# Routing the second head of the first expert group between the first five gathered rows

## The chip, the core and the metric

One NeuronCore of a Trainium2 chip runs the whole program. The time is the device time of one execution in microseconds; lower is better. The engines are called by their short names: PE is TensorE (matmuls and transposes), DVE is VectorE, ACT is ScalarE, POOL is GpSimd (here it issues the gathers), SP is SyncE (here it issues the plain loads and stores).

## What is computed

One inference step of a one-layer decoder: 256 prompt tokens and 8 x 4 sample tokens go through a recurrent head group, a sparse attention group, a cross-attention into 256 memory tokens and, last, a retrieval from 16384 single-neuron experts. The change lies in the last part and in the cross-attention of the second prompt tile. For every token and each of 8 heads the two halves of a query are scored against 128 keys, the 16 best of each half give 256 sums, the 16 best of these name 16 experts, and the rows of two tables are gathered by those numbers:

```
    qh = (x @ w_q).reshape(n, PEER_HEADS, 2, PEER_KEY_DIM)
    s = jnp.einsum('nhcd,hckd->nhck', qh, sub_keys).astype(jnp.float32)
    s1, i1 = lax.top_k(s[:, :, 0], PEER_TOPK)
    s2, i2 = lax.top_k(s[:, :, 1], PEER_TOPK)
    ...
    top_s, j = lax.top_k(cand, PEER_TOPK)
    e = jnp.take_along_axis(cidx, j, axis=-1)
    gate = jax.nn.softmax(top_s, axis=-1)
    h = jax.nn.gelu(jnp.einsum('nd,nhkd->nhk', x, u_tab[e]).astype(jnp.float32))
    return jnp.einsum('nhk,nhkd->nd', (gate * h).astype(x.dtype), v_tab[e])
```

## The kernel before

Tokens lie on the 128 partitions: prompt tile 0, prompt tile 1, and one tile of sample tokens. The expert part is cut into 9 groups (`NGRP`) of 32 picks (`PICK`), that is two heads of one tile each; groups 0 to 3 are tile 0, 4 to 7 tile 1, 8 the sample tokens. One pick is a "row": POOL gathers one row of `peer_u` for each of the 128 tokens (512 KB, 4 KB a token) into one of 6 slots (`USLOTS`), DVE multiplies it with the tokens and sums (L1327, result in `hcur`), and frees the slot (`u_free`). The rows of `peer_v` are gathered into 10 slots a group later, and PE adds them up with the weights `wz` (L1836), four rows a step.

Every engine has its own program, and the order on each is written out by hand. On DVE, PE, ACT and POOL a loop over a row number n runs beside the rest of the layer. On the first three it is a generator, `peer()`, and `stream.upto(step)` in the other code runs it until rows 0 to step - 1 are done. A table (`SIDE`) gives each piece of other work, called by its key, the row number at which it stands; `filled(engine, key)` and `pace(engine, key)` run the rows up to there and then wait for the key's bank. So ("mw", 1, c), the output projection of tile 1's cross-attention, stands at 13: rows 0 to 12 come ahead of it.

Routing a group (`experts`) is a generator too. It runs on DVE in small steps: `best16` on the scores, sums, `best16` again, then the expert numbers are put together by comparing with `iota16` (`eqm`, `ef`) and written as integers `Ei` (which POOL's gathers of u read) and four times as `E4`. Its arguments say which heads; with one head it has 25 steps. `e_half` tells POOL that head 0 of group 0 is there (rows 0 to 15), `e_ready` that the rest is. While the rows of group g are worked on, group g + 1 is routed between them, some steps a row.

The numbers for `peer_v` are needed turned: PE transposes `E4` into bank 2 and counts `et_full`, and DVE copies it into `ETi` (L1349) and counts `eti_ready`. POOL issues the gathers in one order: u0 to u16, v0, u17, v1, u18 and so on to v9, then u alone up to the second group. Ahead of v0 it waits for `eti_ready` and for the bank of ("mw", 1, 1), since the v slots lie over weights that this product reads.

The cross-attention of tile 1 runs in the same time: PE makes the scores ("ms", 1, k); DVE takes their maximum (`mem_max(1)`); ACT takes the exponentials straight from the banks (`mem_exps(1)`) and, behind that in its own order, the copies of the query block (0, 1) that PE waits for; DVE divides (`mem_weighted(1)`); PE turns the result, multiplies it with the values, and then with `w_mem_o` ("mw"). When ("mw", 1, 1) is done, SP loads the next 2 MB of `peer_w_q` into the same buffer, and the query block (0, 2) waits for that. `residual("mw", 1)` and `norm` on DVE end the cross-attention.

Of the kernel before, what the change touches and what calls it, by code (L numbers as in the profile page):

```python
# [38 lines left out]
NGRP = 9  # L39
# [260 lines left out]
def layer_kernel(nc, A, O):  # L300
# [145 lines left out]
    def vload(m):  # L446

        kind, k, use = V_PLACES[m][:3]
        return (s_u if kind == "u" else s_v)[k], 16 * use
# [79 lines left out]
    def bc(ap, axis, n):  # L529

        v = ap.unsqueeze(axis)
        shape = list(v.shape)
        shape[axis] = n
        return v.to_broadcast(shape)

    def split(ap, n):
        return ap.rearrange("p (a b) -> p a b", b=n)

    def toks(t):
        return TILES[t]  # L540
# [675 lines left out]
    def _(dve):  # L1216
# [99 lines left out]
        def peer():  # L1316

            route = None
            for n in range(NSTEP + PICK + 8):
                g, k = n // PICK, n % PICK  # L1320
                if n < NSTEP:
                    if n == 8 * PICK:
                        dve.wait_ge(s_rep, 48)
                    if k == 0 and g >= 2:
                        dve.wait_ge(gelu_done, g - 1)
                    dve.wait_ge(s_u[n % USLOTS], 16 * (n // USLOTS + 1))
                    v.tensor_tensor_reduce(out=uslot[n % USLOTS][:, :], in0=uslot[n % USLOTS][:, :], in1=xt[:, g // 4, :], scale=1.0, scalar=0.0,  # L1327
                                           op0=ALU.mult, op1=ALU.add, accum_out=hcur[:, g % 2, k:k + 1]).then_inc(u_free, 1)
                if 1 <= g <= NGRP:
                    o = g - 1  # L1330
                    if k == 1:
                        dve.wait_ge(gelu_done, o + 1)
                        if o >= 1:
                            dve.wait_ge(wt_full, o)
                        v.tensor_tensor(w4[:, :, :], bc(gcur[:, :], 1, 4), bc(Wg[:, o % 2, :], 1, 4), ALU.mult).then_inc(w4_done, 1)
                    if k == 3:
                        dve.wait_ge(wt_full, o + 1)
                        if o >= 2:
                            dve.wait_ge(v_done, 8 * (o - 1))
                        turned = bc(split(psum[:, 2, 128:256], 32), 1, 8)  # L1340
                        v.tensor_tensor(wz[:, o % 2], turned, bc(C("vmask", 32), 2, 4), ALU.mult).then_inc(wz_done, 1)
                if k == (10 if g else 12) and g < NGRP:
                    dve.wait_ge(et_full, g + 1)
                    if g >= 2:
                        dve.wait_ge(v_done, 8 * (g - 1))
                    for a in range(4):
                        rows = slice(32 * a, 32 * a + 32)
                        src = psum[rows, 2, 0:128].rearrange("p (j i a) -> p a i j", j=4, a=4)[:, a]
                        v.tensor_copy(ETi[rows, g % 2, :].rearrange("p (i j) -> p i j", j=4), src).then_inc(eti_ready, 1)  # L1349
                if g < NGRP - 1:  # L1350
                    start, last, each = (17, 24, 6) if g == NGRP - 2 else (4, 20, 3)
                    if k == start:
                        route = experts(g + 1)
                    if start <= k < last:
                        for _ in range(each):
                            next(route, None)
                    if k == last:
                        for _ in route:
                            pass
                    if n == 10:  # L1360
                        gates(0)
                    if k == 30:
                        gates(g + 1)
                for t in range(2):
                    if n == 4 * PICK * (t + 1) + PICK + 4:
                        dve.wait_ge(v_done, 32 * (t + 1))
                        for c in range(2):
                            x = xt[:, t, GW * c:GW * c + GW]
                            ins = v.scalar_tensor_tensor(out=x, in0=x, scalar=ALPHA, in1=psum[:, c, :], op0=ALU.mult, op1=ALU.add)
                            V(ins, y_free, wait=(c == 1))  # L1370
                        norm(t, small3, s_lnv3, s_lnr3, t + 1, lnp, (s_lnp, 64), s_ln3)
                yield
# [75 lines left out]
        for t in range(3):  # L1448
            t0, n = toks(t)
# [140 lines left out]
        affine(0)  # L1590
        for r in range(2):
            copy_first(dve, r)
            for _ in experts(0, r, 1):
                pass
        mem_max(1)


# [141 lines left out]
                            V(ins, wait=False)  # L1739
                release(dve, ins, key)  # L1740

        stream.upto(1)
        mem_weighted(1)
        residual("mw", 1)
        norm(1, small[:, 170:190], s_lnv, s_lnr, 4, None, None, s_ln)
# [56 lines left out]
    def _(pe):  # L1802
        mm, tr = nc.tensor.matmul, nc.tensor.transpose

        def peer():

            for n in range(NSTEP + PICK + 8):
                g, k = n // PICK, n % PICK
                if k == (8 if g else 1) and g < NGRP:
                    pe.wait_ge(e_ready, 2 * g + 2)  # L1810
                    if g == 0:
                        pe.wait_ge(bank_free[2], USED[2])
                    else:
                        pe.wait_ge(eti_ready, 4 * g)
                    tr(psum[:, 2, 0:128], E4[:, :, :].rearrange("p a k -> p (a k)"), ident).then_inc(et_full, 1)
                if k == 2 and 1 <= g <= NGRP:
                    pe.wait_ge(w4_done, g)
                    if g >= 2:
                        pe.wait_ge(wz_done, g - 1)
                    tr(psum[:, 2, 128:256], w4[:, :, :].rearrange("p a k -> p (a k)"), ident).then_inc(wt_full, 1)  # L1820
                m = n - PICK - 5
                if m >= 0 and m % VB == 0 and m < NSTEP:
                    o, i = m // PICK, m % PICK // VB
                    t, first, last = o // 4, o % 4 == 0 and i == 0, (o % 4 == 3 or o == 8) and i == 7
                    if i == 0:
                        pe.wait_ge(wz_done, o + 1)
                    if m == 0:
                        for b in range(2):
                            pe.wait_ge(bank_free[b], USED[b])
                    elif first:  # L1830
                        pe.wait_ge(y_free, 2 * t)
                    for j in range(4):
                        pe.wait_ge(*vload(m + j))
                    for c in range(2):
                        for j in range(4):
                            ins = mm(psum[32 * j:32 * j + 32, c, :], wz[:, o % 2, i, j, :], vbuf(m + j)[:, GW * c:GW * c + GW],  # L1836
                                     start=first, stop=last)
                    ins.then_inc(v_done, 1)
                yield
# [160 lines left out]
        for t in range(3):  # L2000
            n = toks(t)[1]
# [584 lines left out]
```

## Time and profile before

| what | us |
|---|---|
| median of 3 runs | 1323.2 (1322.02 to 1329.27) |
| the profiled execution, whole | 1328.25 |
| its span, first to last instruction | 1326.5 |
| PE busy | 845.0 (64%) |
| DVE busy | 721.3 (54%) |
| POOL busy | 659.3 (50%) |
| ACT busy | 224.6 (17%) |
| moved by DMA | 428.52 MB, mean 323 GB/s |

The busy shares are means over stages that differ much. Up to about 330 us the program is a chain of matmuls; the gathers begin at 334 us and run to the end.

### The profile page before, as it was taken

To read this page: it belongs to the slowest core of one execution; us is meant where nothing else is said; L and a number is where in the kernel's file an instruction comes from. 1 tells how busy PE (TensorE), PEld (TensorE's weight loads), DVE (VectorE), ACT (ScalarE), POOL (GpSimd) and SP (SyncE) were. 2 spreads that over 40 slices of the span, in tenths; PEclk is the share of its full clock that TensorE was granted. 3 is DMA by queue.
4 is the path that set the end of the run, shared out by engine and by line. 5 is a ranking of instruction groups with operands and counts; after the bars stand their busy time and mean duration, and the time that the engine had idled before them with its cause. 6 is when DMAs were issued, how large, how long until landed. Compare 5 with 4: busy or idle time off the path is not lost.

```text
span 1326.5 us, 12915 instructions
## 1 busy us (share of the span) xinstructions
PE 845.0 (64%) x4547; PEld 436.6 (33%) x4547; DVE 721.3 (54%) x1816; ACT 224.6 (17%) x433; POOL 659.3 (50%) x631
## 2 busy tenths in 40 slices
PE   7999899998857878778544543265444334523344
PEld 5666654545523355455312211022031111100000
DVE  1233673215995944656984783496276253764431
ACT  2211441111302233120111110121121011100000
POOL 4000100000566677666677776457565455577772
PEclk9999899999979989997776767677687677656578
DMA  6874233741699899999999999999999999999995
GB/s 217 215 219 128 72 127 97 284 158 64 204 361 403 310 410 411 408 383 400 347 381 409 409 407 358 372 411 410 415 410 407 404 394 409 358 371 374 391 380 235
DMA packets 145055, 428.52 MB, mean 323 GB/s; under 512 B 26080, under 2 KB 33696, under 8 KB 141664
## 3 DMA queue, kind: packets, MB, share of 16 engines
q0 software_dynamic: 87168, 318.82, 62.3%
q1 hardware_dynamic: 57824, 108.89, 23.6%
q8 instruction: 37, 0.61, 0.2%
q14 instruction: 26, 0.21, 0.0%
HBM read 420.74 MB, written 6.52 MB: 322 GB/s over the span
## 4 chain that ended last, share of the span: by engine, by line
PE 35%; DMA 25%; POOL 23%; issue 9%; DVE 4%; ACT 2%; SPq 0%; POOLq 0%; DVEq 0%; ACTq 0%
PE banks L1896 18%; DMA u<-in_peer_u,Ei 12%; POOL v L844 11%; POOL u L844 11%; DMA v<-in_peer_v,ETi 8%; PE banks L1836 4%; PE banks L1903 2%; DMA wbuf<-in_w_in 2%; DMA ws<-in_peer_w_q 2%; DVE u L1327 1%; DMA wbuf<-in_peer_w_q 1%; POOL slv L844 1%; ACT subg L1101 1%; PE banks L2060 1%; DVE sstate L1627 1%
## 5 line engine op out<-in xcount | busy, mean ns | idle before, releaser
L1327 DVE CUSTOM_DVE_ANT_0 u<-u,xt 128x1024 f32<-128x1024 f32 x288 | 351.8, 1224 | 324.8 <-DMA u<-in_peer_u,Ei 321.3
L844 POOL DMA_INDIRECT u<-in_peer_u,Ei x288 | 301.4, 1047 | 393.0 <-DVE Ei L1304 191.9
L1836 PE MATMUL banks<-v,wz 128*32 128x512 f32 x1104 | 210.7, 887 | 288.8 <-DMA v<-in_peer_v,ETi 253.4
L844 POOL DMA_INDIRECT v<-in_peer_v,ETi x276 | 303.8, 1101 | 109.2 <-issue 85.2
L1836 PEld LDWEIGHTS banks<-v,wz 128*32 128x32 f32 x1104 | 42.2, 141 | 394.6 <-issue 374.0
L859 POOL TENSOR_TENSOR z<-z,par 128x512 f32<-128x512 f32 x2 | 2.5, 1292 | 123.7 <-ACT zs L995 123.7
L2266 PE MATMUL banks<-subT,w1s 128*128 128x252 f32 x256 | 59.2, 388 | 5.9 <-issue 4.5
L1896 PE MATMUL banks<-wbuf,x2T 128*128 128x512 f32 x112 | 51.8, 617 | 14.6 <-DMA wbuf<-in_peer_w_q 11.9
L1896 PE MATMUL banks<-wbuf,memT 128*128 128x512 f32 x128 | 55.9, 593 | 0.0
L2266 PEld LDWEIGHTS banks<-subT,w1s 128*128 128x128 f32 x256 | 48.7, 194 | 18.7 <-issue 11.4
L1896 PE MATMUL banks<-wbuf,xT 128*128 128x512 f32 (+1 forms) x128 | 49.7, 546 | 1.5 <-DMA wbuf<-in_w_in 1.5
L1896 PEld LDWEIGHTS banks<-wbuf,x2T 128*128 128x128 f32 x112 | 21.7, 199 | 42.9 <-issue 42.9
L1896 PEld LDWEIGHTS banks<-wbuf,memT 128*128 128x128 f32 x128 | 24.1, 190 | 28.9 <-issue 28.7
L1896 PEld LDWEIGHTS banks<-wbuf,xT 128*128 128x128 f32 x128 | 24.1, 190 | 25.9 <-issue 22.4
L1903 PE MATMUL banks<-xT,wbuf 128*128 128x288 f32 x128 | 31.6, 408 | 0.0
L1896 PE MATMUL banks<-wbuf,mixT 128*128 128x512 f32 x64 | 27.9, 594 | 1.6 <-issue 1.6
L1896 PE MATMUL banks<-wbuf,mixTm 128*128 128x512 f32 x64 | 27.9, 594 | 1.4 <-issue 1.4
L1896 PE MATMUL banks<-wbuf,x1T 128*128 128x512 f32 x64 | 28.0, 592 | 0.0
L2254 PE MATMUL banks<-cst,subg 128*128 128x128 f32 x128 | 18.3, 298 | 14.4 <-ACT subg L1101 14.4
L504 ACT ACTIVATE KTm<-banks 128x512 f32<-128x512 f32 x32 | 16.8, 602 | 61.0 <-PE banks L2474 61.0
L1903 PEld LDWEIGHTS banks<-xT,wbuf 128*128 128x128 f32 x128 | 24.2, 190 | 8.2 <-issue 1.7
L941 ACT ACTIVATE gcur<-hcur 128x32 f32<-128x32 f32 x9 | 2.1, 229 | 137.5 <-DVE hcur L1327 137.4
(459 smaller groups left out, 1260.6 us busy)
## 6 DMA issues: line engine op xcount, KB each, us to landing
wbuf<-in_w_in SPq DMA_DIRECT2D x4, 2048.0 KB, 15.8
wbuf<-in_peer_w_q SPq DMA_DIRECT2D x4, 2048.0 KB, 10.2
mck<-in_cache_mem_k SPq DMA_DIRECT2D x8, 1024.0 KB, 17.7
mcv<-in_cache_mem_v SPq DMA_DIRECT2D x8, 1024.0 KB, 13.0
ws<-in_peer_w_q SPq DMA_DIRECT2D x4, 2048.0 KB, 19.9
u<-in_peer_u,Ei POOLq DMA_INDIRECT x288, 9.9
v<-in_peer_v,ETi POOLq DMA_INDIRECT x276, 10.0
wbuf<-in_w_mem_k SPq DMA_DIRECT2D x2, 2048.0 KB, 8.4
```

What stands on the lines that cost most here:

```text
L504: ins = nc.scalar.activation(dst, src, ACT.Copy, scale=1.0 if scale is None else scale)
L844: return nc.gpsimd.indirect_dma_start(out=dst, out_offset=None, in_=table, in_offset=bass.IndirectOffsetOnAxis(ap=index, axis=0)).then_inc ...
L859: nc.gpsimd.tensor_tensor(gate, gate, bc(hng[0:n], 1, H), ALU.mult).then_inc(s_gz, 1)
L1101: nc.scalar.copy(subg[:, :, :, :], sub[f % 3][:, :].rearrange("p (s g d) -> p g s d", s=16, g=2)).then_inc(s_sorted, 1)
L1327: v.tensor_tensor_reduce(out=uslot[n % USLOTS][:, :], in0=uslot[n % USLOTS][:, :], in1=xt[:, g // 4, :], scale=1.0, scalar=0.0, op0=ALU.mu ...
L1627: ins = v.scalar_tensor_tensor(out=sstate[:, b, h, :], in0=sstate[:, b, h, :], scalar=dec[:, h, NCH + b:NCH + b + 1], in1=bank(key)[:, P * ...
L1836: ins = mm(psum[32 * j:32 * j + 32, c, :], wz[:, o % 2, i, j, :], vbuf(m + j)[:, GW * c:GW * c + GW], start=first, stop=last)
L1896: ins = mm(o[0:n, 0:w], xs[:, k, t0:t0 + n], wt[:, k, 0:w], start=(k == 0), stop=(k == KC - 1))
L1903: ins = mm(o[:, 0:n], wt[:, k, cols:cols + P], xs[:, k, 0:n], start=(k == 0), stop=(k == KC - 1))
L2060: ins = mm(o[:, K * i:K * i + K], qn[r, h % 4, t0:t0 + P], kn[r, br, 0:K], start=True, stop=True)
L2254: ins = tr(o[:, P * m:P * m + P], rows[:, D * g:D * g + D].rearrange("p (k c) -> p c k", c=8)[:, c, :], ident)
L2266: ins = mm(split(o[:, 0:4 * NCB], NCB), w1s[:, n, :], part, start=(n == 0), stop=(n == 15))
```

## The change

Before, DVE routes head 0 and then head 1 of group 0 in one go, takes the maximum for tile 1's softmax, and only then begins with the rows. Now it routes head 0, and row 0 follows after nine steps of head 1, rows 1 to 4 each after five more (the last step comes ahead of row 4). `mem_max(1)` comes after row 2 instead of ahead of row 0, `mem_weighted(1)` after row 3 instead of after row 0. The transposition of `E4` for group 0 on PE moves from row 1 to row 12, the copy into `ETi` on DVE from row 12 to row 14, and the routing of group 1 begins at row 6 instead of row 4. Nothing is added or left out.

```
--- before.py
+++ after.py
@@ -1318,6 +1318,14 @@
             route = None
             for n in range(NSTEP + PICK + 8):
                 g, k = n // PICK, n % PICK
+                if n == 0:
+                    route = experts(0, 1, 1)
+                if n < 5:
+                    for _ in range(5 if n else 9):
+                        next(route, None)
+                if n == 5:
+                    for _ in route:
+                        pass
                 if n < NSTEP:
                     if n == 8 * PICK:
                         dve.wait_ge(s_rep, 48)
@@ -1339,7 +1347,7 @@
                             dve.wait_ge(v_done, 8 * (o - 1))
                         turned = bc(split(psum[:, 2, 128:256], 32), 1, 8)
                         v.tensor_tensor(wz[:, o % 2], turned, bc(C("vmask", 32), 2, 4), ALU.mult).then_inc(wz_done, 1)
-                if k == (10 if g else 12) and g < NGRP:
+                if k == (10 if g else 14) and g < NGRP:
                     dve.wait_ge(et_full, g + 1)
                     if g >= 2:
                         dve.wait_ge(v_done, 8 * (g - 1))
@@ -1348,7 +1356,7 @@
                         src = psum[rows, 2, 0:128].rearrange("p (j i a) -> p a i j", j=4, a=4)[:, a]
                         v.tensor_copy(ETi[rows, g % 2, :].rearrange("p (i j) -> p i j", j=4), src).then_inc(eti_ready, 1)
                 if g < NGRP - 1:
-                    start, last, each = (17, 24, 6) if g == NGRP - 2 else (4, 20, 3)
+                    start, last, each = (17, 24, 6) if g == NGRP - 2 else (4 if g else 6, 20, 3)
                     if k == start:
                         route = experts(g + 1)
                     if start <= k < last:
@@ -1590,8 +1598,9 @@
         affine(0)
         for r in range(2):
             copy_first(dve, r)
-            for _ in experts(0, r, 1):
-                pass
+        for _ in experts(0, 0, 1):
+            pass
+        stream.upto(3)
         mem_max(1)
 
 
@@ -1739,7 +1748,7 @@
                             V(ins, wait=False)
                 release(dve, ins, key)
 
-        stream.upto(1)
+        stream.upto(4)
         mem_weighted(1)
         residual("mw", 1)
         norm(1, small[:, 170:190], s_lnv, s_lnr, 4, None, None, s_ln)
@@ -1806,7 +1815,7 @@
 
             for n in range(NSTEP + PICK + 8):
                 g, k = n // PICK, n % PICK
-                if k == (8 if g else 1) and g < NGRP:
+                if k == (8 if g else 12) and g < NGRP:
                     pe.wait_ge(e_ready, 2 * g + 2)
                     if g == 0:
                         pe.wait_ge(bank_free[2], USED[2])
```

How DVE's program reads at the first rows and at the softmax of tile 1, before the change. `ISA u` is a row (L1327), followed by the reading of its sum; `Ei` and `E` end the routing of head 1; `small<-banks` at L1566 is the maximum; `Pmt` is the softmax of tile 1:

```order
L1301 SCALAR_TENSOR_TENSOR Ef<-ef 128x16 [waits dve_step]
L1304 CAST Ei<-Ef 128x16 [waits dve_step]
L1306 COPY E_157<-Ef 128x128
L1566 TENSOR_REDUCE small<-banks 128x2 [waits bank_full6]
L1566 TENSOR_REDUCE small<-banks 128x2 [waits bank_full7,dve_step]
L1567 TENSOR_SCALAR small<-small 128x4 [waits dve_step]
L1327 ISA u_126,hcur<-u_126,xt 128x1024 [waits s_u0,s_mmx]
L1327 ISA hcur 128x1
```

The same place after it, from the last routing step ahead of row 2 to row 3:

```order
L1293 TENSOR_TENSOR eqm<-jaf,cst 128x256 [waits dve_step]
L1335 ISA u_128,hcur<-u_128,xt 128x1024 [waits s_u2,dve_step]
L1335 ISA hcur 128x1
L1574 TENSOR_REDUCE small<-banks 128x2 [waits bank_full6]
L1574 TENSOR_REDUCE small<-banks 128x2 [waits bank_full7,dve_step]
L1575 TENSOR_SCALAR small<-small 128x4 [waits dve_step]
L1297 TENSOR_TENSOR eqm<-eqm,tif 128x256 [waits s_mmx]
L1299 TENSOR_REDUCE ef<-eqm 128x16 [waits dve_step]
L1293 TENSOR_TENSOR eqm<-jaf,cst 128x256 [waits dve_step]
L1297 TENSOR_TENSOR eqm<-eqm,tif 128x256 [waits dve_step]
```

The maximum stood behind the whole routing and ahead of row 0; it now stands behind row 2, with routing steps on both sides of it.

DVE's program at the end of tile 1's cross-attention, before. The first `ISA u` is row 12, `CAST ETi` is the copy that POOL's v0 waits for, L1226 is the residual, which waits for the banks of ("mw", 1, 0) and ("mw", 1, 1):

```order
L1327 ISA u_126,hcur<-u_126,xt 128x1024 [waits s_u0,dve_step]
L1327 ISA hcur 128x1
L1349 CAST ETi<-banks 32x32 [waits et_full]
L1349 CAST ETi<-banks 32x32 x3
L1263 MAX_INDEX cj<-cv,cand 128x8 x2
L1265 MATCH_REPLACE cand<-cv,cand 128x256 [waits dve_step]
L1226 SCALAR_TENSOR_TENSOR xt<-xt,banks 128x512 [waits bank_full5]
L1226 SCALAR_TENSOR_TENSOR xt<-xt,banks 128x512 [waits bank_full6,bank_free5]
```

After, from the last operation of the norm (L1240), seven places behind the first residual, to the copy; the two `ISA u` with tiles are rows 13 and 14:

```order
L1240 TENSOR_SCALAR xt<-xt,small 128x1024 [waits dve_step]
L1335 ISA u_127,hcur<-u_127,xt 128x1024 [waits s_u1,s_ln]
L1335 ISA hcur 128x1
L1281 TENSOR_TENSOR cand<-tv 128x256
L1261 MAX cv<-cand 128x8 [waits dve_step]
L1261 MAX cv<-cand 128x8
L1335 ISA u_128,hcur<-u_128,xt 128x1024 [waits s_u2,dve_step]
L1335 ISA hcur 128x1
L1357 CAST ETi<-banks 32x32 [waits et_full]
L1357 CAST ETi<-banks 32x32 x3
```

The copy stood two places ahead of the residual; it now stands behind the residual, the norm and two rows.

## Rows read from the trace of the kernel before

**Rows 1.** the page, part 2: mean busy share of the DMA engines, in tenths, 40 slices

```profile
DMA  6874233741699899999999999999999999999995
```

**Rows 2.** windows of ten microseconds: busy time by engine, clock, DMA share, GB/s

```profile
420.00:430.00 10.00, 8.44 (x29) 4.09 (x28) 3.76 (x7) 3.30 (x5) 5.79 (x6) 1.00 1.03 411
430.00:440.00 10.00, 8.68 (x34) 3.40 (x34) 8.97 (x30) 0.60 (x1) 4.60 (x3) 0.83 0.80 286
440.00:450.00 10.00, 8.44 (x41) 3.81 (x40) 8.31 (x28) 1.79 (x3) 8.29 (x6) 1.00 0.82 263
450.00:460.00 10.00, 8.44 (x41) 3.76 (x39) 9.79 (x24) 2.66 (x4) 7.56 (x9) 1.00 0.97 344
```

**Rows 3.** timeline, POOL: start, us, line, transfer, idle before and what ended it

```profile
333.85 1.06 POOL L844 DMA_INDIRECT u<-in_peer_u,Ei  x1 [191.89 <-DVE Ei L1304]
...
346.29 0.94 POOL L844 DMA_INDIRECT u<-in_peer_u,Ei  x1 [5.08 <-DVE hcur L1327]
349.79 1.68 POOL L844 DMA_INDIRECT u<-in_peer_u,Ei  x1 [2.56 <-DVE hcur L1327]
...
366.88 1.34 POOL L844 DMA_INDIRECT u<-in_peer_u,Ei  x1 [0.30 <-issue]
372.71 0.94 POOL L844 DMA_INDIRECT v<-in_peer_v,ETi  x1 [4.50 <-issue]
```

**Rows 4.** the tile u, 330 to 372 us: time from issue to landing

```profile
DMA to landing us min/median/max: 4.2/5.6/6.4
```

**Rows 5.** timeline, DVE, end of the first routing, softmax of tile 1, first row

```profile
332.81 0.17 DVE L1304 CAST Ei<-Ef 128x16 int32<-128x16 f32 x1
...
343.14 1.41 DVE L1566 TENSOR_REDUCE small<-banks 128x2 f32<-128x512 f32 x2
...
344.79 1.23 DVE L1327 CUSTOM_DVE_ANT_0 u<-u,xt 128x1024 f32<-128x1024 f32 x1
...
347.03 1.22 DVE L1574 TENSOR_TENSOR Pmt<-Pmt,small 128x1024 f32<-128x1024 f32 x1
```

**Rows 6.** timeline, ACT, softmax of tile 1 and the copy behind it

```profile
344.79 0.47 ACT L1058 ACTIVATE Pmt<-banks,small 128x256 f32<-128x256 f32 x1 [5.84 <-DVE small L1567]
...
348.40 0.60 ACT L504 ACTIVATE pqst<-banks 128x512 f32<-128x512 f32 x1 [1.56 <-PE banks L1896]
```

**Rows 7.** timeline, PE, from the turned softmax to the first query block with the new weights

```profile
351.62 1.04 PE L2167 MATMUL banks<-cst,Pmt 128*128 128x128 f32 x8
...
357.97 13.97 PE L1896 MATMUL banks<-wbuf,mixTm 128*128 128x512 f32 x32 [0.72 <-issue]
383.89 9.20 PE L1896 MATMUL banks<-wbuf,x2T 128*128 128x512 f32 x16 [11.95 <-DMA wbuf<-in_peer_w_q]
```

**Rows 8.** timeline, DVE, around the residual of tile 1

```profile
369.72 0.84 DVE L1349 CAST ETi<-banks 32x32 int32<-32x32 f32 x4
...
371.97 1.41 DVE L1226 SCALAR_TENSOR_TENSOR xt<-xt,banks 128x512 f32<-128x512 f32 x2
...
376.69 1.23 DVE L1327 CUSTOM_DVE_ANT_0 u<-u,xt 128x1024 f32<-128x1024 f32 x1
...
379.14 1.23 DVE L1327 CUSTOM_DVE_ANT_0 u<-u,xt 128x1024 f32<-128x1024 f32 x1
```

**Rows 9.** DMA issues, 290 to 320 us: one weight load with few others

```profile
wbuf<-in_peer_w_q SPq DMA_DIRECT2D x1, 2048.0 KB, 8.1
```

**Rows 10.** timeline, DVE, rows 31 and 35 and the first wz

```profile
415.96 1.23 DVE L1327 CUSTOM_DVE_ANT_0 u<-u,xt 128x1024 f32<-128x1024 f32 x1 [2.79 <-DMA u<-in_peer_u,Ei]
...
424.15 1.22 DVE L1327 CUSTOM_DVE_ANT_0 u<-u,xt 128x1024 f32<-128x1024 f32 x1
...
430.93 1.23 DVE L1341 TENSOR_TENSOR wz<-banks,cst 128x1024 f32<-128x1024 f32 x1 [5.54 <-PE banks L1820]
```

**Rows 11.** timeline, ACT, gelu of group 0 and the copy behind it

```profile
422.54 0.23 ACT L941 ACTIVATE gcur<-hcur 128x32 f32<-128x32 f32 x1
427.50 0.60 ACT L504 ACTIVATE pqst<-banks 128x512 f32<-128x512 f32 x1 [4.73 <-PE banks L1896]
```

More of the change, by code:

```diff
@@ L1320, in peer @@
                 g, k = n // PICK, n % PICK
+                if n == 0:
+                    route = experts(0, 1, 1)
+                if n < 5:
+                    for _ in range(5 if n else 9):
+                        next(route, None)
+                if n == 5:
+                    for _ in route:
+                        pass
                 if n < NSTEP:
@@ L1341, in peer @@
                         v.tensor_tensor(wz[:, o % 2], turned, bc(C("vmask", 32), 2, 4), ALU.mult).then_inc(wz_done, 1)
-                if k == (10 if g else 12) and g < NGRP:
+                if k == (10 if g else 14) and g < NGRP:
                     dve.wait_ge(et_full, g + 1)
@@ L1350, in peer @@
                 if g < NGRP - 1:
-                    start, last, each = (17, 24, 6) if g == NGRP - 2 else (4, 20, 3)
+                    start, last, each = (17, 24, 6) if g == NGRP - 2 else (4 if g else 6, 20, 3)
                     if k == start:
@@ L1592, in _ @@
             copy_first(dve, r)
-            for _ in experts(0, r, 1):
-                pass
+        for _ in experts(0, 0, 1):
+            pass
+        stream.upto(3)
         mem_max(1)
@@ L1740, in mem_sample @@
                 release(dve, ins, key)
-        stream.upto(1)
+        stream.upto(4)
         mem_weighted(1)
@@ L1808, in peer @@
                 g, k = n // PICK, n % PICK
-                if k == (8 if g else 1) and g < NGRP:
+                if k == (8 if g else 12) and g < NGRP:
                     pe.wait_ge(e_ready, 2 * g + 2)
```

## Prediction

> **What bounds the kernel now.** I read the DMA line of the page first, because the gathers are most of the bytes: from the eleventh slice (332 us) it rises, and from the fifteenth to the last but one it stands at 9 throughout [rows 1]. In windows the full level is 1.03 and 411 GB/s [rows 2]. So the second two thirds of the program run at the rate of the DMA engines, and a change at their head moves the end only by the DMA time that it wastes or fills before that stretch is full. The windows name the one hole left inside: from 430 to 460 us the share is 0.80, 0.82 and 0.97 [rows 2]. Against 1.03 that is (0.23 + 0.21 + 0.06) x 10 / 1.03 = 4.9 us of idle DMA time.
>
> Then I read the engines' timelines from 333 to 380 us, to see who holds the gathers back at the start. POOL issues u0 at 333.85, waits for DVE's rows ahead of u6 (5.08 us, until 346.29) and u7 (2.56 us, until 349.79), issues the rest to u16 at 366.88, and then stands 4.50 us until v0 goes out at 372.71 [rows 3]. What ended last there is no semaphore that the view names. DVE's copy into ETi ran from 369.72 to 370.56 [rows 8], while the matmuls of ("mw", 1, 1) ended at 357.97 + 13.97 = 371.94 [rows 7], 0.77 us before v0. So the product on PE opens the gate of v0 now, and the copy is 1.4 us early. POOL works in order, so u17 and all that follows wait at the same gate.
>
> **The change part by part.** Durations are from the one profiled execution, which took 1328.25 us with a span of 1326.5; that is 5.0 above the median of the three runs, and I carry the difference over to the median.
>
> *Rows 0 to 2 earlier.* Head 1's 25 steps lie between 332.98 (end of head 0's Ei) and 343.14 (first maximum) [rows 5], 0.41 us a step. Nine steps end at 336.7. Row 0 needs its gather: issued at 333.85 [rows 3], and gathers here landed 4.2 to 6.4 us after issue [rows 4], so at 338.1 to 340.2, instead of the present start at 344.79 [rows 5]. DVE idles 1.4 to 3.6 us, which it did not before. u6 and u7 can go out about 5 us earlier. I book nothing for it: u16 and v0 stand behind in POOL's order, and the gate at 372 us is not moved by it. If v0 were free, the gain would be those 5 to 7 us; it is a rival below.
>
> *The softmax of tile 1 later.* From row 0 to the maximum there are now three rows (1.2 us each [rows 5]) and ten steps (4.1 us): 7.7 us behind 338.1 to 340.2, so 345.8 to 347.9 instead of 343.14, 2.7 to 4.8 us later. Behind the maximum on ACT are the exponentials and, in order, the copy that PE's query block (0, 1) waits for. ACT was ready for this copy 1.56 us before it could begin at 348.40 [rows 6], so the copy comes 1.1 to 3.2 us later. PE's queue behind it is: two more turns of the block, the turned softmax (351.62), the values, and ("mw", 1) [rows 7]. All are dense there, so the product ends as much later; I take the middle, 2.1 us: 374.0 instead of 371.94. The division (mem_weighted) begins after five more steps and row 3, at 350.7 to 352.8, and takes 1.4 us; PE asks for it at 351.62 + 1.1 to 3.2 = 352.7 to 354.8, so it is covered by about half a microsecond.
>
> *DVE at the residual.* Before, DVE came there at 371.97 [rows 8]. Six routing steps of group 1 (2.5 us) and the ETi copy (0.84) now lie behind it, the idle time at row 0 lies ahead: 371.97 - 3.3 + 1.4 to 3.6 = 370.1 to 372.3. The product ends at 374.0, so DVE's own delay is hidden, with 1.7 us to spare at the worse end.
>
> *The ETi copy.* This is the dearest part. Before, from the two residuals to row 13 took 376.69 - 371.97 = 4.72 us, of which 0.7 is the first residual [rows 8]; now only the second is behind the product: 374.0 + 4.0 = 378.0 for row 13. Row 14 comes 2.45 us later as now (379.14 - 376.69; the steps between are others of like size), ends at 381.7, and the copy at 382.5. With the 0.77 us that POOL took from its gate to the gather, v0 goes out at 383.3 instead of 372.71: 10.6 us later, 9.5 to 11.7 with the ends above. The transposition on PE at row 12 costs nothing: E4 is written about 353, and PE comes to row 12 only after the values, at about 359.
>
> *What lies in the gap.* The weight load behind ("mw", 1, 1) is 2.10 MB, 5.1 us of DMA time at 411 GB/s. In the trace it shared the engines with the gathers and PE got it after 11.95 us [rows 7]; a load of the same size with little beside it landed 8.1 us after issue [rows 9]. So it lands at 374.0 + 8.1 = 382.1 instead of 383.89, and the query blocks on PE may start 1.8 us earlier. I book none of that, for the reason in the next part. The gathers have then only lost 10.6 - 5.1 = 5.5 us of DMA time (4.4 to 6.6).
>
> *Who is late next.* At the full level this is a lag of 5.5 us for rows 20 to 35. Row 31 began at 415.96 and row 35 ended at 424.15 + 1.2 = 425.4 [rows 10]; then DVE stood 5.54 us until 430.93, for PE, which does the first w4 only behind the query block (1, 2) [rows 10]. Row 35 will end at 430.9. The stall covers the lag and 1.8 us of a faster PE could not be used, since row 35 is not there earlier. From then on POOL and DVE go as before, and the DMA engines work off the lag in their 4.9 us of idle time up to 460 us [rows 2]. What is left is 5.5 - 4.9 = **0.6 us** (-0.5 to 1.7).
>
> Sum: 1328.25 + 0.6 = 1328.9 for such an execution, 1323.2 + 0.6 = 1323.8 for the median; I say 1324.
>
> *A rule that speaks against the change.* The gathers issued beside no rows took 0.94 to 1.06 us on POOL, the one at 349.79, with rows on DVE beside it, 1.68 [rows 3]. The Trainium skill, "SBUF — State Buffer" (Who interferes with whom), says that some VectorE operations hold a port pair that GpSimd needs, so that GpSimd cannot write descriptors until they end; this trace agrees in direction. By that rule the rows now put between u3 and u6 would stretch these gathers by 0.74 us each, 2.2 us in all, DVE would come to the residual at up to 374.5, and the upper end of the remainder would be 0.5 higher.
>
> **The rivals.** *Slower: the lag is not absorbed.* The 5.5 us pass the stall only while row 35 ends by 430.9, and there is no margin in that; each microsecond beyond goes one to one into the order behind it. A second place is ACT: its gelu of group 0 needs row 31 and stands ahead of the copy of block (1, 2) at 427.50, on which PE's chain hangs [rows 11]. Row 31 would end at 417.2 + 5.5 = 422.7, and the gelu takes 0.23, so this decides only from a lag of 10 us. For it speaks that the DMA engines may not fill their idle time, since POOL is slow to issue beside the routing. Price: 5.5 us if the idle time is not used, up to 10.6 if v0's whole delay stays: 1328.7 to 1333.8.
>
> *Faster: v0 is not late.* If the copy or the product came as early as now, the earlier slots would count: 4.8 us at u6 (346.29 against about 341.5), up to 6.6 at u7 (349.79 against 343.2), so 1318.4 to 1316.6. Against it stands the order on DVE, which puts the copy behind the residual, and that the DMA hole of 4.9 us is the most there is to fill. It decides if v0 goes out by 372.7.
>
> *Nothing of it is seen:* both ends are small, and the result is what the forecast says for another reason, such as the faster PE chain (1.8 us) setting the pace from 430 us: 1322.
>
> **How the numbers follow.** The forecast has 0.60 (own range 1320 to 1327, the remainder of -0.5 to 1.7 and the spread of the runs), the slower rival 0.20, the faster one 0.13, the last 0.07. About 0.5% (6.6 us) is what a measurement of this kernel can tell from no change. Of the slower rival's 5.5 to 10.6 somewhat over half lies beyond 6.6, with the spread of the runs 0.16 is slower. The faster rival only reaches that bound; with the spread half of it counts, and some for a stretch that I misjudged: 0.11. The rest, 0.73, is the same. The range leaves out the outer halves of both rivals: 1316 to 1332.
>
> **What would show it.** Right: row 0 at 338 to 340 and u6 before 343; the maximum at 346 to 348; ("mw", 1, 1) ending near 374; the ETi copy at 382; v0 near 383 with POOL idle over 12 us ahead of it; the next query block starting by 383; wz at about 431; a DMA share near 1.0 from 430 to 445. Wrong: v0 by 373 (then faster), or wz after 433 with the share still low from 440 to 460 (then slower).

## The result, and the profile after

| | before | after |
|---|---|---|
| median, 20 runs each, same chips | 1326.53 | 1333.02 |
| profiled span | 1326.5 | 1333.6 |
| first gather of u issued | 333.85 | 334.03 |
| v0 issued | 372.71 | 386.19 |
| first wz | 430.93 | 440.17 |

The ratio is 1.0059 (95% interval 1.0041 to 1.0078): 5.4 to 10.3 us slower, where the forecast had 0.6. 0.0059 of 1326.5 is 7.8 us (the two medians alone differ by 6.5), inside the slower rival's price of 5.5 to 10.6; whether its reasons came in too is weighed further down. The forecast's 1324 started from the median of 3 runs, 1323.2; 20 runs put that at 1326.53, so 3.3 us of the distance from 1324 to 1333.02 are no part of the change.

POOL's timeline of the changed kernel, for [rows 3]; the bracket is the idle time ahead and what ended it:

```profile
334.03 1.06 POOL L844 DMA_INDIRECT u<-in_peer_u,Ei  x1 [192.41 <-DVE Ei L1304]
...
341.87 0.93 POOL L844 DMA_INDIRECT u<-in_peer_u,Ei  x1 [0.30 <-issue]
343.40 0.93 POOL L844 DMA_INDIRECT u<-in_peer_u,Ei  x1 [0.60 <-DVE hcur L1335]
...
365.80 0.94 POOL L844 DMA_INDIRECT u<-in_peer_u,Ei  x1 [0.30 <-issue]
386.19 0.93 POOL L844 DMA_INDIRECT v<-in_peer_v,ETi  x1 [19.45 <-DVE ETi L1357]
387.43 1.82 POOL L844 DMA_INDIRECT u<-in_peer_u,Ei  x1 [0.30 <-issue]
...
412.54 0.97 POOL L844 DMA_INDIRECT v<-in_peer_v,ETi  x1 [0.31 <-issue]
```

The early slots came as forecast: u6 and u7 went out 4.4 and 6.4 us earlier. Then POOL stood 19.45 us instead of 4.50, for the copy into `ETi`. The last two rows are u17 and v9, which went out 26.35 us behind v0.

DVE, for [rows 5, 8, 10]: row 0, the maximum, the second residual, row 14, the copy, row 15, row 25, row 31, wz:

```profile
338.30 1.22 DVE L1335 CUSTOM_DVE_ANT_0 u<-u,xt 128x1024 f32<-128x1024 f32 x1 [2.52 <-DMA u<-in_peer_u,Ei]
...
346.37 1.41 DVE L1574 TENSOR_REDUCE small<-banks 128x2 f32<-128x512 f32 x2
...
377.65 0.69 DVE L1226 SCALAR_TENSOR_TENSOR xt<-xt,banks 128x512 f32<-128x512 f32 x1 [6.25 <-PE banks L1905]
...
383.93 1.22 DVE L1335 CUSTOM_DVE_ANT_0 u<-u,xt 128x1024 f32<-128x1024 f32 x1
...
385.08 0.84 DVE L1357 CAST ETi<-banks 32x32 int32<-32x32 f32 x4
...
387.22 1.22 DVE L1335 CUSTOM_DVE_ANT_0 u<-u,xt 128x1024 f32<-128x1024 f32 x1
...
421.80 1.22 DVE L1335 CUSTOM_DVE_ANT_0 u<-u,xt 128x1024 f32<-128x1024 f32 x1 [6.00 <-DMA u<-in_peer_u,Ei]
...
433.33 1.22 DVE L1335 CUSTOM_DVE_ANT_0 u<-u,xt 128x1024 f32<-128x1024 f32 x1
...
440.17 1.23 DVE L1349 TENSOR_TENSOR wz<-banks,cst 128x1024 f32<-128x1024 f32 x1
```

Row 31 is 17.4 us later, and the stall of 5.54 us ahead of wz is gone, since wz itself is 9.2 us later. Row 25 waits 6.00 us for its gather where it waited 1.32 us before: the rows are shorter of data than they were.

ACT, for [rows 6, 11]: exponentials, copy of block (0, 1), gelu of group 0, copy of block (1, 2):

```profile
348.01 0.47 ACT L1058 ACTIVATE Pmt<-banks,small 128x256 f32<-128x256 f32 x1 [8.88 <-DVE small L1575]
...
350.09 0.60 ACT L504 ACTIVATE pqst<-banks 128x512 f32<-128x512 f32 x1
...
434.60 0.23 ACT L941 ACTIVATE gcur<-hcur 128x32 f32<-128x32 f32 x1 [9.20 <-DVE hcur L1335]
434.74 0.58 ACT L504 ACTIVATE pqst<-banks 128x512 f32<-128x512 f32 x1
```

PE, for [rows 7], and the wait behind ACT:

```profile
350.83 1.05 PE L2211 MATMUL banks<-cst,pqst 128*128 128x128 f32 x4 [2.34 <-ACT pqst L504]
352.66 2.05 PE L2216 MATMUL banks<-skT,pqT 128*128 128x128 f32 x8 [0.78 <-ACT pqT L504]
354.50 1.91 PE L2176 MATMUL banks<-cst,Pmt 128*128 128x128 f32 x8
357.15 5.71 PE L2186 MATMUL banks<-PTmp,mvt 128*128 128x128 f32 x32 [0.73 <-issue]
...
363.58 13.97 PE L1905 MATMUL banks<-wbuf,mixTm 128*128 128x512 f32 x32 [0.61 <-issue]
385.93 10.04 PE L1905 MATMUL banks<-wbuf,x2T 128*128 128x512 f32 x16 [8.38 <-DMA wbuf<-in_peer_w_q]
...
435.46 1.09 PE L2211 MATMUL banks<-cst,pqst 128*128 128x128 f32 x4 [5.12 <-ACT pqst L504]
```

The copy came 1.7 us later, but ("mw", 1, 1) ended at 377.55, 5.6 us later. The turned softmax took 1.91 us where it took 1.04 [rows 7]. The clock that was granted to PE from 350 to 360 us was 0.54 of full speed in the mean (1.00 before): from 352 to 360 us it read 0.50, the lower of its two levels (1.2 GHz of 2.4).

Now the bytes. Windows of ten microseconds counted from each kernel's first gather of u, from 40 us on; the last two columns are DMA share and GB/s. Before:

```profile
373.85:383.85 10.00, 0.00 (x0) 0.00 (x0) 9.22 (x26) 0.20 (x1) 7.76 (x8) 0.53 1.03 398
383.85:393.85 10.00, 9.20 (x16) 3.75 (x16) 9.79 (x21) 0.60 (x1) 7.88 (x7) 0.79 1.03 410
393.85:403.85 10.00, 6.49 (x29) 4.03 (x30) 5.38 (x11) 3.99 (x10) 8.16 (x7) 1.00 1.03 409
403.85:413.85 10.00, 8.44 (x29) 4.25 (x28) 7.38 (x15) 3.19 (x5) 7.56 (x9) 1.00 1.02 391
413.85:423.85 10.00, 8.44 (x28) 4.10 (x28) 4.75 (x8) 3.30 (x5) 4.59 (x5) 1.00 1.03 403
423.85:433.85 10.00, 7.12 (x34) 3.33 (x36) 4.46 (x11) 1.79 (x3) 3.85 (x4) 0.93 1.03 417
433.85:443.85 10.00, 9.22 (x30) 3.41 (x23) 9.86 (x37) 0.60 (x1) 7.48 (x5) 0.90 0.69 206
443.85:453.85 10.00, 9.22 (x43) 4.30 (x42) 8.24 (x20) 1.19 (x2) 8.06 (x7) 1.00 0.88 315
453.85:463.85 10.00, 6.97 (x48) 3.94 (x46) 9.72 (x29) 5.65 (x9) 6.96 (x8) 1.00 1.01 373
463.85:473.85 10.00, 3.62 (x18) 3.20 (x19) 5.07 (x11) 4.16 (x5) 7.79 (x8) 0.64 1.03 412
```

After:

```profile
374.03:384.03 10.00, 3.52 (x9) 1.25 (x7) 5.73 (x13) 0.20 (x1) 0.00 (x0) 0.88 0.54 182
384.03:394.03 10.00, 8.10 (x12) 3.48 (x13) 8.29 (x26) 0.00 (x0) 6.32 (x6) 0.61 0.61 198
394.03:404.03 10.00, 5.73 (x28) 3.46 (x27) 9.33 (x22) 4.58 (x11) 7.87 (x8) 1.00 1.01 371
404.03:414.03 10.00, 8.44 (x29) 4.13 (x28) 3.70 (x6) 3.18 (x5) 7.87 (x8) 1.00 0.90 326
414.03:424.03 10.00, 8.44 (x29) 4.23 (x28) 2.47 (x4) 1.73 (x4) 5.81 (x6) 1.00 1.04 405
424.03:434.03 10.00, 6.31 (x15) 2.47 (x13) 7.32 (x14) 1.36 (x2) 5.13 (x6) 0.94 0.95 350
434.03:444.03 10.00, 5.93 (x28) 3.20 (x29) 9.35 (x18) 1.91 (x4) 7.87 (x8) 0.50 0.97 341
444.03:454.03 10.00, 9.22 (x28) 3.73 (x20) 8.80 (x35) 0.60 (x1) 8.17 (x7) 0.88 0.99 401
454.03:464.03 10.00, 9.22 (x42) 4.21 (x40) 8.64 (x20) 1.19 (x2) 8.06 (x7) 1.00 1.03 404
464.03:474.03 10.00, 6.81 (x47) 3.87 (x45) 9.73 (x29) 5.81 (x9) 6.92 (x8) 1.00 0.99 367
```

The first two rows of after move 182 + 198 against 398 + 410: 428 GB/s over 10 us is 4.28 MB, 10.4 us at 410 GB/s. The next four move 1452 against 1620, another 4.1 us. So at 100 us behind the first gather the changed kernel is **14.5 us of transfers behind**. In the next three (the hole around the first wz) it moves 1146 against 894 and wins 6.1 us back; the tenth loses 1.1 again: 9.5. (Counted from the first gather on, as in the table below, the 14.5 are 14.7.) Row 63 of DVE, counted from the first gather, is 9.1 us later. This account of bytes is the measure in all that follows.

### The profile page after: what moved, and what is told of

The parts are those of the page before. It is cut to its first block, busy times and chain, and to the rows that moved or that the text cites. A ratio compares the mean times of both kernels' runs of the same rounds, so it can differ in the third digit from the quotient of the medians.

```text
span 1333.6 us, 12916 instructions
## 1 busy us (share of the span) xinstructions
PE 850.4 (64%) x4547; PEld 444.2 (33%) x4547; DVE 721.9 (54%) x1816; ACT 225.2 (17%) x433; POOL 651.7 (49%) x631
## 4 chain that ended last, share of the span: by engine, by line
PE 31%; DMA 27%; POOL 23%; issue 10%; DVE 7%; ACT 2%; SPq 0%; POOLq 0%; DVEq 0%; ACTq 0%
DMA u<-in_peer_u,Ei 17%; PE banks L1905 15%; POOL v L844 12%; POOL u L844 11%; DMA v<-in_peer_v,ETi 6%; PE banks L1845 3%; PE banks L1912 2%; DMA wbuf<-in_w_in 2%; DVE u L1335 2%; DMA ws<-in_peer_w_q 2%; PE banks L2263 1%; POOL slv L844 1%; PE banks L2186 1%; PE banks L2069 1%; ACT subg L1101 1%
## 5 line engine op out<-in xcount | busy, mean ns | idle before, releaser
L844 POOL DMA_INDIRECT u<-in_peer_u,Ei x288 | 296.3, 1029 | 393.2 <-DVE Ei L1304 192.4
L1226 DVE SCALAR_TENSOR_TENSOR xt<-xt,banks 128x512 f32<-128x512 f32 (+1 forms) x12 | 8.2, 682 | 37.9 <-PE banks L1905 37.7
L2263 PE MATMUL banks<-cst,subg 128*128 128x128 f32 x128 | 18.8, 304 | 14.5 <-ACT subg L1101 14.5
## 6 DMA issues: line engine op xcount, KB each, us to landing
u<-in_peer_u,Ei POOLq DMA_INDIRECT x288, 10.3
v<-in_peer_v,ETi POOLq DMA_INDIRECT x276, 10.4
```

The costliest lines, as they stand in the source:

```text
L844: return nc.gpsimd.indirect_dma_start(out=dst, out_offset=None, in_=table, in_offset=bass.IndirectOffsetOnAxis(ap=index, axis=0)).then_inc ...
L1226: release(dve, v.scalar_tensor_tensor(out=x, in0=x, scalar=ALPHA, in1=bank((name, t, c))[0:n], op0=ALU.mult, op1=ALU.add), (name, t, c), w ...
L2263: ins = tr(o[:, P * m:P * m + P], rows[:, D * g:D * g + D].rearrange("p (k c) -> p c k", c=8)[:, c, :], ident)
```

## The experiments

The theory at first (T): v0 is late for two reasons, the copy's place and the late product on PE, and POOL's order hands that on in full. The rivals: the interleaving of routing and rows costs it (R1), or the late softmax alone (R2).

Each ran next to the kernel before (12 timed runs each, 17 to 35 of before). "Behind" is the account of bytes against before, in us at 410 GB/s, at 100 and at 200 us behind the first gather; "row 63" is its lag on that clock; v0 and ("mw", 1, 1)'s end are us behind the first gather. These come from one execution each, the ratio from the timed runs. The last line is a second execution of the changed kernel: it ends 10.8 us behind where the first ended 9.5, with row 63 11.1 late and not 9.1, so a difference of 1 to 2 us in the columns behind v0's can be chance. There is no E9.

| kernel | mw ends | v0 | behind at 100 | at 200 | row 63 | ratio, 95% interval |
|---|---|---|---|---|---|---|
| before | 38.1 | 38.9 | 0 | 0 | 0 | 1 |
| after | 43.5 | 52.2 | 14.7 | 9.5 | 9.1 | 1.0059 [1.0041, 1.0078] |
| E1 after, copy at 12 | 43.7 | 44.5 | 5.3 | 4.8 | 5.2 | 1.0008 [0.9985, 1.0031] |
| E2 after, softmax earlier | 38.0 | 46.7 | 9.3 | 4.0 | 3.9 | 1.0042 [1.0021, 1.0064] |
| E3 both of these | 38.0 | 38.8 | -0.3 | 0.4 | 0.3 | 1.0007 [0.9981, 1.0033] |
| E4 before, copy at 14 | 38.1 | 46.8 | 8.6 | 1.6 | 1.7 | 1.0012 [0.9985, 1.0038] |
| E5 before, softmax late | 44.0 | 44.8 | 5.7 | 5.1 | 5.0 | 1.0036 [1.0009, 1.0063] |
| E6 after, PE's gap filled | 41.3 | 49.9 | 12.3 | 7.7 | 7.6 | 1.0037 [1.0007, 1.0067] |
| E7 before, w4 turned first | 38.1 | 38.9 | -0.1 | 1.7 | 1.3 | 1.0001 [0.9975, 1.0028] |
| E8 after, gelu later | 39.5 | 48.2 | 11.0 | 7.0 | 6.5 | 1.0070 [1.0041, 1.0098] |
| E10 before, sums first | 38.1 | 38.9 | 0.4 | 3.2 | 3.2 | 1.0040 [1.0009, 1.0070] |
| E11 E3, sums first | 38.0 | 38.8 | -0.1 | 3.3 | 3.6 | 1.0023 [0.9992, 1.0054] |
| E12 E10, pages later | 38.1 | 38.9 | -0.3 | 4.6 | 4.4 | 1.0046 [1.0026, 1.0066] |
| after, once more | 43.7 | 52.3 | 14.6 | 10.8 | 11.1 | one run, 1331.85 us |

**E1 to E4: the parts of the change.** E1 undoes one number, E2 two, E3 both; E4 puts one number into the kernel before.

E1, DVE's copy into `ETi`:

```
-                if k == (10 if g else 14) and g < NGRP:
+                if k == (10 if g else 12) and g < NGRP:
```

E2, ahead of `mem_max(1)` and of `mem_weighted(1)`:

```
-        stream.upto(3)
+        stream.upto(2)
...
-        stream.upto(4)
+        stream.upto(3)
```

E4 is E1's line the other way round (12 becomes 14), in the kernel before.

> The changed kernel with VectorE's copy of the first group's indices back at row 12 (ahead of the second tile's residual and norm) and all else as changed. T (the gathers from the value table are paced by GpSimd's issue order, so that whatever v0 comes later is handed on in full; 7.9 of its 13.5 us are the copy's place, 5.6 the late softmax): the product of the memory read still ends near 377.5 us, v0 is issued near 378.3 instead of 386.2, row 31 comes some 8 us earlier than 433.3, and ScalarE's gelu of group 0 no longer holds the query block's copy by several us; 1.002 to 1.004 of the kernel before. R1 (the interleaving of routing and first rows is itself what costs): 1.005 to 1.006. R2 (the late softmax alone costs it, through TensorE): 1.006.

> The changed kernel with the second tile's row maximum put two rows (instead of three) behind the first, and its weighting one row later, so that the softmax is as early as the interleaved rows let it be; the copy stays at row 14. T: TensorE's turns of the softmax find no long idle time ahead of them, the product of the memory read ends near 372 us, v0 is issued near 382.3; 1.003 to 1.005. R1: 1.005 to 1.006, since the interleaving is unchanged. R2: 1.000, since TensorE's chain is as before.

> The changed kernel with both: the row maximum one row earlier, and the copy of the indices back at row 12. What is left of the change is the routing of the second head between the first rows. T: v0 near 372.7 us as in the kernel before, row 31 near 416, 0.998 to 1.002. R1: 1.005.

> The kernel before with one number changed: VectorE's copy of the first group's indices at row 14 (behind the second tile's residual, norm and rows 12 and 13) instead of row 12. Softmax and routing as before. T: v0 near 381.5 us instead of 372.7, the gathers from the value table shifted by the same all along, row 31 later than 416 by 8 to 12 us, VectorE's stall at wz gone but ScalarE's gelu standing ahead of the query block's copy; 1.003 to 1.005. R1 and R2: 1.000, since neither the interleaving nor the softmax is changed.

v0's delay came apart as T said: the copy's place alone 7.8 and 7.9 us (E2, E4), the softmax alone 5.6 (E1; 5.9 in E5 below), both 13.3, neither 0 (E3). R1 falls with E3: the routing between the first rows costs nothing by itself. R2 falls with E2. But T's second half, that v0's delay is handed on in full, falls with E4: row 63 is only 1.7 us late. E4 lost 8.6 us of transfers and won 7.0 back around wz, where the kernel before has its hole; E1 lost 5.3 and won only 0.5 back. (E4's ratio lies below T's 1.003 to 1.005, but its interval reaches 1.0038, so it is the trace that decides.) The difference is PE. In E4 the weights behind ("mw", 1, 1) landed while the gathers stood, and PE's chain of query blocks was 3.4 us early; in E1 that chain is 6.3 us late, the turn of w4 at its end as well, and the hole stays. E1's timeline of DVE has the stall of before unchanged:

```profile
436.29 1.23 DVE L1349 TENSOR_TENSOR wz<-banks,cst 128x1024 f32<-128x1024 f32 x1 [5.54 <-PE banks L1829]
```

E1's ratio is lower than its account: 4.8 us are 1.0036. In its profiled execution the last wz is only 2.2 us behind, so some of the 4.8 was given back in the later groups; what did that was not looked for.

**E5: the late softmax alone,** in the kernel before.

```
+        stream.upto(3)
         mem_max(1)
...
-        stream.upto(1)
+        stream.upto(4)
         mem_weighted(1)
```

> The kernel before with only the second tile's softmax three rows later: its row maximum behind row 2 and its weighting one row after that; routing ahead of the rows and the copy at row 12, as before. Revised theory T2, from the four runs above (in the first 100 us behind the first gather the transfers move fewer bytes than before; what is not refilled into the idle stretch that the kernel before has around its first wz is the loss): TensorE's turns of the softmax stand behind a gap and at a lower granted clock, the memory read's product ends up to 5.6 us later, v0 and the next query block's weights come 5 us later, the deficit is 4 to 5.5 us and the idle stretch around wz stays, since wz is as late as the rest; 1.002 to 1.004. Rival R1 (the interleaving of the routing is what costs): 1.000, as the routing is untouched.

The ratio is 1.0036, inside T2's range, with 5.1 us behind at 200 us, and R1 falls a second time. Behind a gap of 2.74 us on PE the turns took 1.09, 2.04 and 1.92 us.

**E6: PE's gap filled,** to see what the clock costs. The products' results are overwritten by the turns.

```
             o = begin(("pqT", t, q))
+            if (t, q) == (0, 1):
+                for _ in range(5):
+                    mm(o[:, :], x2T[0][:, 0, :], landed(WG["peer_w_q", 1])[:, 0, :], start=True, stop=True)
             evacuated(pe, ("pq", t, q))
```

> The changed kernel with five added products of 128x128 by 128x512 on TensorE between the query block (0,1) and its turns, into a bank that the turns overwrite; they stand where TensorE otherwise waits for ScalarE's copy. If the idle gap of 2.34 us is what takes the granted clock down behind it: the clock of 350 to 360 us stays near 1.0, the eight turns take 0.63 and 1.13 us instead of 1.05 and 2.05, the product of the memory read ends near 374.5 instead of 377.6, v0 comes near 383 instead of 386.2, the deficit of bytes falls by 3 us; 1.003 to 1.005. If the clock falls for another reason, the product still ends near 377.6 and the ratio stays at 1.006.

The turns were back at 0.60, 1.13 and 1.04 us, v0 came 2.3 us sooner than after's, the account ends at 7.7 instead of 9.5. E8 below, where the clock stayed up by itself, ends at 7.0; the second execution of the changed kernel, where it fell again, at 10.8. So by two executions against two the lower clock cost some 2 to 3 us of the 9.5. The ratio's interval overlaps that of the changed kernel and can't show so little by itself.

**E7 and E8: two queue orders near the first wz.**

E7 in `SIDE`, E8 at ACT's gelu:

```
-    (quad_jobs(1, 0), 22, 23), (quad_jobs(1, 1), 28, 29), (quad_jobs(1, 2), 34, 34),
+    (quad_jobs(1, 0), 22, 23), (quad_jobs(1, 1), 28, 29), (quad_jobs(1, 2), 36, 36),
```

```
-                if k == 0 and 1 <= g <= NGRP:
+                if k == (4 if g == 1 else 0) and 1 <= g <= NGRP:
```

> The kernel before with the query block (1,2) planned at step 36 instead of 34, so that TensorE turns w4 ahead of that block. T2: VectorE's stall of 5.54 us at the first wz goes, wz comes at 424 to 426 instead of 430.9, the gathers do not run out of buffers, and the transfers' idle stretch of 430 to 460 us (8 us at the pace around it) is filled; 0.995 to 0.998. If that stretch is hidden behind something else: 1.000, with another wait behind wz.

> The changed kernel with ScalarE's gelu of the first group behind its copies of the query block (1,2) instead of ahead of them, so that TensorE's block does not stand behind row 31. Two readings of why the changed kernel is late at its first wz. If the queue order on ScalarE decides (the recorded rival's second place): TensorE's wait of 5.12 us goes, the query block ends 2.7 us later than before instead of 9, and the ratio falls to 1.001 to 1.003. T2 (the bytes not moved decide: row 31 itself lands 17 us later, and w4 needs it): wz comes at 437 to 438 instead of 440.2, the deficit stays near 9 us; 1.004 to 1.006.

E8: PE's wait of 5.12 us went, and nothing was gained (1.0070). DVE's w4 needs row 31 itself, and row 31 stands behind rows that wait for their bytes (it is 13.4 us late here, counted from the first gather). So the gelu's place on ACT is where the lag shows, not what causes it; the account's 7.0 us, 1.0053, lie inside the ratio's interval.

E7 failed the other way: wz came 5.6 us earlier, DVE's stall was gone, and the time stayed. POOL's timeline shows the wait that took its place: the value buffers come free only with PE's sums, and these now stood behind the moved block.

```profile
438.79 1.13 POOL L844 DMA_INDIRECT v<-in_peer_v,ETi  x1 [6.72 <-PE banks L1836]
```

**E10, E11, E12: can the hole be filled at all?** The sums ahead of the block too; in E12 two page gathers later as well.

E10 and E11, and what E12 has besides, in POOL's order:

```
-    (quad_jobs(1, 0), 22, 23), (quad_jobs(1, 1), 28, 29), (quad_jobs(1, 2), 34, 34),
-    (quad_jobs(0, 3), 38, 38), (quad_jobs(1, 3), 42, 43),
+    (quad_jobs(1, 0), 22, 23), (quad_jobs(1, 1), 28, 29), (quad_jobs(1, 2), 38, 38),
+    (quad_jobs(0, 3), 42, 42), (quad_jobs(1, 3), 46, 46),
```

```
+        cmp_at[3:5] = [55, 57]
```

> The kernel before with three query blocks planned later: (1,2) at step 38, (0,3) at 42, (1,3) at 46 instead of 34, 38 and 42, so that the turn of w4 and the first sums of the value rows stand ahead of block (1,2) on TensorE, and the buffers of the value rows come free earlier. T2: in the run with the turn alone ahead, GpSimd's wait for a buffer of the value rows kept the idle stretch; now the first sum comes near 427 instead of 432.2, GpSimd's wait of 5 us goes, the transfers' idle stretch of 430 to 460 us (7 to 8 us at the pace around it) is filled; 0.995 to 0.998. If the stretch is bound by something else: 1.000 again.

> The same three query blocks later, on the kernel that keeps of the change only the routing between the first rows (copy at row 12, row maximum one row earlier). T2: as the run above, 0.995 to 0.999, since that kernel had the same idle stretch and no deficit; if the routing between the rows costs something that the idle stretch hid, 1.5 to 3 us more than the run above.

> The run with the sums ahead of the block, with the gathers of the fourth and fifth compressed page put at steps 55 and 57 of GpSimd's order instead of 50 and 52, since GpSimd stood there for 13.24 us behind ScalarE's copy of the first page. T2: the stretch around the first wz stays filled (row 47 some 4 us earlier than in the kernel before), the wait at the page's gather goes or shrinks to a few us, and the account of bytes ends 2 to 4 us ahead of the kernel before; 0.997 to 0.999. If TensorE's row of three query blocks with the value sums between them (12.3 us each for four rows) is the next bound: GpSimd waits for a buffer of the value rows instead, and the ratio is 1.000 to 1.003.

All three missed. E10 is 3.6 us of transfers ahead at 120 us, and then POOL stands for the fourth compressed page, whose buffer ACT frees only behind the last query block. In E12 that wait is gone, the kernel is 5.1 us ahead at 130 us, and POOL then stands for PE's sums. POOL's timeline, E10 and then E12:

```profile
468.82 0.94 POOL L844 DMA_INDIRECT sub<-in_cache_k_cmp,idx  x1 [13.24 <-ACT subg L1101]
```

```profile
478.99 0.94 POOL L844 DMA_INDIRECT v<-in_peer_v,ETi  x1 [11.69 <-PE banks L1837]
```

In these orders the hole of the kernel before is therefore not free DMA time: PE's row of query blocks makes it, and the block that is put off makes it again later. The second reading of E12's expectation (PE's blocks as the next bound) names this wait, but its 1.000 to 1.003 is below the 1.0046 measured and only touches the interval's lower end. No version here beats the kernel before.

**The changed kernel once more,** for the clock.

> The changed kernel as it is, profiled once more, for the granted clock behind TensorE's gap near 350 us: in the first profile it fell to 0.54 behind a gap of 2.34 us, in the run with the gelu behind the copies it did not behind one of 2.30 us. If the gap of that length decides it, the turns take 1.05, 2.05 and 1.91 us again and the product of the memory read ends 43.5 us after the first gather; if it varies between executions, they may take 0.63, 1.13 and 1.04 and the product ends near 39.5.

It repeats: a gap of 2.49 us, turns of 0.99, 2.05 and 1.91, the product 43.7 us behind the first gather, v0 at 52.3, 14.6 behind at 100 us and 10.8 at 200.

## Why the prediction was wrong, point by point

*Rows 0 to 2 earlier.* Right: row 0 at 338.30 (338.1 to 340.2), u6 before 343, and no gain from it.

*The softmax later.* The maximum (346.37) and the copy (+1.7) came in their ranges. The term "All are dense there, so the product ends as much later; I take the middle, 2.1 us" was mis-sized: 5.6. Of this 1.7 is the copy, and 3.9 the work behind it, from 8.83 us (349.14 to 357.97) to 12.75 (350.83 to 363.58) at the lower clock. In E8, whose program is the changed one up to there, the clock did not fall and the product was 1.4 us late, near the forecast. I took durations from a PE that had not stood idle.

*The copy's place.* Right: v0 8.6 us behind the product (forecast 9.3).

*What lies in the gap: "The gathers have then only lost 10.6 - 5.1 = 5.5 us of DMA time".* **This step failed.** It takes the gathers behind v0 to run at the DMA engines' full rate, so that a load moved out of their way gives its 5.1 us back. They don't: from v0 to v9 POOL issues 18 gathers in 26.35 us, 1.46 us each (26.57 us before, 25.3 to 27.5 in all fourteen traces), which is 358 GB/s. Before, the load filled the rest up to 410; now it ran in the gap. Thirty us from v0 on, before and then after:

```profile
372.71:382.71 10.00, 0.00 (x0) 0.00 (x0) 9.29 (x24) 0.20 (x1) 7.87 (x8) 0.59 0.98 356
382.71:392.71 10.00, 8.82 (x16) 3.75 (x16) 9.69 (x23) 0.00 (x0) 7.87 (x8) 0.73 1.03 411
392.71:402.71 10.00, 5.73 (x28) 3.52 (x28) 6.04 (x12) 4.59 (x11) 8.17 (x7) 1.00 1.03 409
```

```profile
386.19:396.19 10.00, 9.78 (x16) 3.75 (x15) 8.32 (x25) 0.12 (x1) 7.87 (x8) 0.72 0.75 245
396.19:406.19 10.00, 5.95 (x28) 3.84 (x29) 8.51 (x18) 4.46 (x11) 8.17 (x7) 1.00 0.98 372
406.19:416.19 10.00, 8.44 (x29) 4.14 (x28) 3.70 (x6) 3.19 (x5) 7.87 (x8) 1.00 0.93 339
```

POOL (the fifth busy time) is busy for the same 23.9 us in both, and the changed kernel moves 2.2 MB less; the load is 2.10 MB. All six executions with the copy at 14 read alike (230 to 250, 359 to 375 and 336 to 384 GB/s), and all others like before (351 to 360, 409 to 411, 405 to 410). The share of 0.98 beside 372 GB/s is near the full 1.03: the share alone hides it. E4 has this gap and nothing else of the change: v0 was 7.9 us late, which by the prediction's sum costs 7.9 - 5.1 = 2.8 us, and 8.6 were lost. With the 13.3 us that v0 had in the changed kernel that sum gives 8.2; 14.5 were lost, and v9 is 13.1 us late. The slower rival names this pace ("POOL is slow to issue beside the routing"), but as a reason for the idle stretch at 430 us and not for this one.

*Who is late next.* "The stall covers the lag" failed by its own condition: it held up to a lag of 5.5. The rival's second place, ACT's gelu ahead of the copy from a lag of 10 us, is what the trace then shows (row 31 17.4 us late, PE waiting 5.12). E8 says it only marks the lag.

*The slower rival.* Its price holds the 7.8 us, but its reasons came in only in part, so the fit is partly luck. The idle time that it left unused was used (6.1 us), v0's delay was 13.3 us and not 10.6, and of the lag of 14.5 us not all was handed on. Of its sign, wz after 433 came (440.17), and the share still low from 440 to 460 did not (0.97 to 1.03).

*The idle DMA time.* 4.9 us were booked as filled and 6.1 were, so this term was, if anything, too low. The 4.9 came from the shares; the bytes of [rows 2] (286, 263 and 344 against 411 GB/s) make the hole 8.3 us. That it could be filled depended on PE's chain being no later than the gathers, which E1 and E5 show: there the chain is late too, and at most 0.6 us was won.

*The rule weighed against the trace.* I put 2.2 us on rows beside the gathers u3 to u6, by the Trainium skill, "SBUF — State Buffer" (Who interferes with whom). The trace agrees with the rule, and the price was wrong. A gather that goes out while a row runs on DVE ends about 0.9 us behind that row's end; one that goes out ahead of a row takes its 0.94 us. u4 went out at 339.15, 0.30 us ahead of the end of row 0, and took 1.18; no row was running when u3, u5 and u6 went out, and they took 0.93 to 0.94: 0.24 us in all. The 1.68 us of my one example are those of a gather that went out 0.35 us into a row; I took it for all of them. The same thing makes the pace that I overlooked behind v0, in both kernels: u17 went out at 387.43, 0.21 us into row 15, and took 1.82. With no row beside it a gather takes 0.94 us and 0.30 to the next, 1.24 and not 1.46.

Open: the span is 7.1 us longer, though row 63 is 9.1 late. Single executions scatter by some us in the 800 us behind it (E3's last wz is 3.8 us early with nothing in it to explain that), so where 2 us came back is not settled. The second execution of the changed kernel has row 63 11.1 us late and a span 3.5 us longer. Also open is why E2 keeps 4.0 us where E4, with v0 as late, keeps 1.6: it may be chance, or the routing between the rows costs something when the copy stands at 14, though it costs nothing by itself (E3).

## What to carry to other kernels

A delay ahead of an in-order queue of transfers is lost in full at first when the queue's own pace is below the rate of the DMA engines: other transfers that are moved into the gap give nothing back, since the queue can't use the rate that they leave. How much of it stays depends on the next idle stretch (E4 won 7.0 of 8.6 us back, E1 0.5 of 5.3). Count the bytes moved in equal windows from a common event, for both kernels: the difference in microseconds at the full rate told the lag of row 63, which stands behind these bytes, in thirteen executions here to 0.5 us, where waits on single engines misled (E7, E8). An idle stretch in the DMA line is only spare if nothing else recreates it a few rows later.

## What the runs showed of the hardware

Gathers issued beside rows on DVE. In the fourteen traces 1299 gathers went out 0.1 to 0.9 us into a row, counted from its start to where the reading of its sum begins, 1.15 us later. Of these 1276 ended 0.75 to 1.0 us behind the row's end: in the median they took 1.86 us when they went out 0.1 to 0.2 us into it, and 1.18 us at 0.8 to 0.9. A row that began while a gather was already under way did not stretch the gather: 1570 such gathers, with DVE idle when they went out, took 0.93 to 0.95 us, all of them. What holds the later one up, no run here shows.

The granted clock behind a short pause of PE. The same stretch of the same program (the changed kernel twice, E1, E8) had gaps of 2.34, 2.49, 2.53 and 2.30 us ahead of its turns: in the first three the granted clock fell to 0.50 (1.2 GHz) and the softmax's turn took 1.91, 1.91 and 1.92 us, in the last it stayed at 1.00 (2.4 GHz) and the turn took 1.04. With 0.84 (E2, E3, E4) or a filled gap (E6) it stayed. The Trainium skill, "TensorE: Matmul & The Clock Gate" (Part 1: The HAM clock gate), says that the clock has two levels and that the point of change varies from run to run; the durations, near twice 1.04, agree with the former, and four executions are too few to say whether the gap's length or chance decided here.
